# The opening of a two-block layer kernel: zero matmuls between the halves of x, short loads on ScalarE's queue, and the first norm's sums moved into the second weight chunk

## The reference, cut to what matters

```
def _rmsnorm(x, w):
    xf = x.astype(jnp.float32)
    y = xf * lax.rsqrt(jnp.mean(xf * xf, axis=-1, keepdims=True) + RMS_EPS)
    return (y * w.astype(jnp.float32)).astype(x.dtype)
...
    h = jnp.concatenate([meta, x], axis=1)
...
    h = h + _mixer(_rmsnorm(h, norm_mix_w[l]), w_in[l], ...)
...
    proj = u @ w_in
    rq, rk, rv, rg, a_cq, a_ckv, a_kr, a_gret, a_gmla = jnp.split(proj, SPLIT_IDX, axis=-1)
```

## Time and profile before

| | |
|---|---|
| time, three runs | 1061.37 us median (1061.02 to 1061.76) |
| the profiled execution | 1061.51 us, span 1059.7 us |
| mean granted TensorE clock | 0.997 |
| busy over the span | PE 1041.0 us, PEld 963.7, DVE 745.9, ACT 548.0, POOL 2.2 |
| HBM read | 174.78 MB, 166 GB/s over the span |

### The profile page before, as it was taken

How to read it: one execution, slowest core, us unless ns; L and a number is a source line. 1 busy time by engine, 2 the same in 40 slices (tenths; PEclk the granted TensorE clock), 3 DMA queues, 4 the chain that set the end, 5 groups by cost and what they waited for, 6 DMA issues and landing times.

```text
span 1059.7 us, 19331 instructions
## 1 busy us (share of the span) xinstructions
PE 1041.0 (98%) x7716; PEld 963.7 (91%) x7716; DVE 745.9 (70%) x810; ACT 548.0 (52%) x589; POOL 2.2 (0%) x5
## 2 busy tenths in 40 slices
PE   8999999999999999999999999999999999999998
PEld 7998997899999999989889999999898997888887
DVE  6855747768766666678767766666788987766673
ACT  6422536545644444465796444444576574444442
POOL 0000000000000000000000000000000000000000
PEclk8999999999999999999999999999999999999999
DMA  9894242345556666666416455465353444646531
GB/s 304 234 205 147 80 140 80 120 140 166 170 173 180 191 195 196 186 201 224 134 41 238 159 195 201 158 207 190 120 160 120 163 156 158 236 160 204 192 119 40
DMA packets 162589, 177.11 MB, mean 167 GB/s; under 512 B 4800, under 2 KB 148288, under 8 KB 162536
## 3 DMA queue, kind: packets, MB, share of 16 engines
q1 hardware_dynamic: 160704, 174.06, 51.5%
q10 hardware_dynamic: 1832, 2.30, 1.2%
HBM read 174.78 MB, written 1.57 MB: 166 GB/s over the span
## 4 chain that ended last, share of the span: by engine, by line
PE 82%; DVE 11%; ACT 4%; issue 1%; DMA 1%; SPq 0%; DVEq 0%; ACTq 0%
PE proj L466 38%; PE aux L910 13%; PE proj L476 11%; PE aux L932 8%; PE proj L475 5%; DVE wlo L1727 4%; DVE f L1727 2%; DVE f L1730 2%; ACT whi L1244 1%; DVE u L1730 1%; PE aux L663 1%; DVE x_all L1727 1%; DMA f<-in_x_dram 1%; PE aux L778 1%; PE aux L763 1%
## 5 line engine op out<-in xcount | busy, mean ns | idle before, releaser
L1727 DVE TENSOR_TENSOR wlo<-raw,whi 128x2048 fp32r<-128x2048 f32 (+2 forms) x179 | 374.6, 2093 | 100.8 <-ACT whi L1244 88.5
L466 PE MATMUL proj<-u,whi 128*128 128x256 f32 (+1 forms) x1888 | 345.4, 285 | 1.5 <-DVE u L1730 0.7
L1244 ACT ACTIVATE whi<-raw 128x2048 fp32r<-128x2048 f32 (+2 forms) x172 | 309.6, 1800 | 69.4 <-PE proj L466 41.9
L466 PEld LDWEIGHTS proj<-u,whi 128*128 128x128 f32 x1888 | 291.5, 189 | 8.3 <-issue 6.5
L466 PE MATMUL proj<-u,wlo 128*128 128x256 f32 (+1 forms) x944 | 266.2, 282 | 0.0
L476 PE MATMUL proj<-u,whi 128*128 128x512 f32 x512 | 179.7, 393 | 0.0
L466 PEld LDWEIGHTS proj<-u,wlo 128*128 128x128 f32 x944 | 178.5, 189 | 0.0
L910 PE MATMUL aux<-v,whi 128*128 128x256 f32 x864 | 154.3, 280 | 0.8 <-DVE v L1727 0.8
L475 PE MATMUL proj<-u,wlo 128*128 128x256 f32 x512 | 143.7, 281 | 0.9 <-DVE u L1730 0.9
L910 PEld LDWEIGHTS aux<-v,whi 128*128 128x128 f32 x864 | 133.0, 188 | 1.9 <-issue 1.2
L910 PE MATMUL aux<-v,wlo 128*128 128x256 f32 x432 | 120.9, 280 | 0.0
(11 more groups left out here) (307 smaller groups left out, 1065.2 us busy)
## 6 DMA issues: line engine op xcount, KB each, us to landing
raw<-in_mlp_w_dram SPq DMA_DIRECT2D x64, 1024.0 KB, 5.5
raw<-in_w_in_dram SPq DMA_DIRECT2D x21, 1024.0 KB, 7.5
raw<-in_od_w_in_dram SPq DMA_DIRECT2D x12, 1024.0 KB, 5.3
raw<-in_w_ffn_gate_dram SPq DMA_DIRECT2D x22, 512.0 KB, 3.9
raw<-in_w_ffn_up_dram SPq DMA_DIRECT2D x22, 512.0 KB, 5.2
raw<-in_w_ffn_down_dram SPq DMA_DIRECT2D x21, 512.0 KB, 5.4
raw<-in_ev_w_in_dram SPq DMA_DIRECT2D x10, 1024.0 KB, 5.5
raw<-in_w_ret_out_dram SPq DMA_DIRECT2D x4, 1024.0 KB, 5.3
```

The lines of the kernel that those rows point to most:

```text
L466: ins = mm(o, w_of(a, k), x_of(b, k), start=first and k == 0 and j == 0, stop=last and k == kt - 1 and j == 2, skip_group_check=skip)
L1244: A.post(act(slot(whi, n, 0, wd), slot(raw, n, 0, wd), ACT.Copy), "hi_ready")
L1727: return ve.tensor_tensor(o, a, b, op)
```

## The change

It does five things, all within the first tens of microseconds:

1. Seven matmuls on zeros (`FILL = 7`, the same instruction as the ten at the start) stand between the turning of k = 3 and of k = 4, ahead of the wait for the right half of x.
2. The 16-row pieces of x (the meta tokens and the tail, of each half) are issued on ScalarE's queue, behind the identity; the parameters follow between the two halves.
3. VectorE keeps the copies of groups 2 and 3 later: the low parts of u and of chunk 0's right half go ahead of them. After chunk 0 it keeps 4 and 5, splits chunk 1, keeps 2, 3, 6 and 7, and splits chunk 2 ahead of the three small operations on the gains.
4. ScalarE squares groups 0 and 1 ahead of chunk 1, groups 4 and 5 ahead of chunk 2, the rest behind it.
5. TensorE's partial sums move from ahead of rq1 to between its two column blocks, and the sum over them from k = 4 of the first block to k = 4 of the second.

```diff
+FILL = 7
@@
             for half, x_sem, w_sem in ((0, "x_left", "first_left"), (1, "x_right", "raw_landed0")):
                 c = slice(512 * half, 512 * half + 512)
-                sp.dma_start(x_tok[0:META, 0, c], meta[:, c]).then_inc(sems[x_sem], 16)
                 sp.dma_start(x_tok[META:P, 0, c], x[0:P - META, c]).then_inc(sems[x_sem], 16)
                 sp.dma_start(x_tok[:, 1, c], x[P - META:2 * P - META, c]).then_inc(sems[x_sem], 16)
-                sp.dma_start(x_tok[0:META, 2, c], x[S - META:S, c]).then_inc(sems[x_sem], 16)
@@
-                                   lambda a, k: src[:, a, k, t0:t0 + t], kt, gate=gate if j == 0 else None)
+                                   lambda a, k: src[:, a, k, t0:t0 + t], kt, gate=gate if j == 0 else late_gate)
@@
             for k in range(KT):
+                if k == 4:
+                    for j in range(FILL):
+                        mm(proj[:, 0, 0:P], warm, warm, start=True, stop=True)
                 if k % 4 == 0:
                     pe.wait_ge(sems["x_right" if k else "x_left"], 64)
@@
-            pe.wait_ge(sems["x_ready"], KT)
-            pe.wait_ge(sems["sq_ready"], 4)
-            for k in range(KT):
-                part = slice(32 * (k % 4), 32 * (k % 4) + 32)
-                ins = mm(aux[part, 0, 0:L], C("ones")[:, 0:32], sq[:, k, :], start=k < 4, stop=k >= 4, skip_group_check=True)
-            ins.then_inc(sems["sum_parts"], 1)
+
+            def token_parts():
+                pe.wait_ge(sems["x_ready"], KT)
+                pe.wait_ge(sems["sq_ready"], 4)
+                for k in range(KT):
...
+                ins.then_inc(sems["sum_parts"], 1)
@@
-            project("rq1", t0=META, t=S, gate=token_sums)
+            project("rq1", t0=META, t=S, between=token_parts, late_gate=token_sums)
@@
-            nc.scalar.dma_start(par[:, :], params).then_inc(sems["par_in"], 16)
+            for half, x_sem in ((0, "x_left"), (1, "x_right")):
+                c = slice(512 * half, 512 * half + 512)
+                nc.scalar.dma_start(x_tok[0:META, 0, c], w["meta_tokens"][:, c]).then_inc(sems[x_sem], 16)
+                nc.scalar.dma_start(x_tok[0:META, 2, c], w["x"][0][S - META:S, c]).then_inc(sems[x_sem], 16)
+                if half == 0:
+                    nc.scalar.dma_start(par[:, :], params).then_inc(sems["par_in"], 16)
@@
+            def token_squares(c, kept):
+                eng.wait_ge(sems["x_ready"], kept)
+                A.post(act(sq[:, 2 * c:2 * c + 2, :], x_all[:, 2 * c:2 * c + 2, :], ACT.Square), "sq_ready")
+
+            token_squares(0, 2)
             pump(index["rq0"] - AHEAD + 1)
-            for c in range(4):
-                eng.wait_ge(sems["x_ready"], 2 * c + 2)
-                A.post(act(sq[:, 2 * c:2 * c + 2, :], x_all[:, 2 * c:2 * c + 2, :], ACT.Square), "sq_ready")
+            token_squares(2, 4)
             pump(index["rq0"] - AHEAD + 2)
+            token_squares(1, 6)
+            token_squares(3, 8)
@@
-            keep(2)
-            keep(3)
             for k in range(4, KT):
                 first_lo(k)
@@
             done[0] = 1
-            for k in range(4, KT):
+            keep(4)
+            keep(5)
+            pump(index["rq0"] - AHEAD + 1)
+            for k in (2, 3, 6, 7):
                 keep(k)
+            pump(index["rq0"] - AHEAD + 2)
             B.run(tt(both_gains, par[:, PAR_COLS["final"][0]:PAR_COLS["final"][0] + KT], both_gains, ALU.mult))
             final_gains = par[:, PAR_COLS["final"][0]:PAR_COLS["final"][0] + KT]
             B.run(tt(gains_and_eps, final_gains, final_gains, ALU.mult))
             B.run(ts(gains_and_eps, gains_and_eps, EPS, ALU.add))
-            pump(index["rq0"] - AHEAD + 2)
```

More of the change, by code:

```diff
@@ L493, in finish, with project @@
                 ins.then_inc(sems["chunk_used"], 1)
-            def project(name, blocks=2, src=u, t0=0, t=L, kt=KT, width=256, m=P, step=P, off=0, gate=None, between=None):
+            def project(name, blocks=2, src=u, t0=0, t=L, kt=KT, width=256, m=P, step=P, off=0, gate=None, between=None,
+                        late_gate=None):
                 n = index[name]
@@ L585, in _ @@
             finish(ins)
-            pe.wait_ge(sems["x_ready"], KT)
-            pe.wait_ge(sems["sq_ready"], 4)
-            for k in range(KT):
-                part = slice(32 * (k % 4), 32 * (k % 4) + 32)
-                ins = mm(aux[part, 0, 0:L], C("ones")[:, 0:32], sq[:, k, :], start=k < 4, stop=k >= 4, skip_group_check=True)
-            ins.then_inc(sems["sum_parts"], 1)
+            def token_parts():
+                pe.wait_ge(sems["x_ready"], KT)
+                pe.wait_ge(sems["sq_ready"], 4)
+                for k in range(KT):
+                    part = slice(32 * (k % 4), 32 * (k % 4) + 32)
+                    ins = mm(aux[part, 0, 0:L], C("ones")[:, 0:32], sq[:, k, :], start=k < 4, stop=k >= 4, skip_group_check=True)
+                ins.then_inc(sems["sum_parts"], 1)
             def token_sums(k):
```

## The result

The changed kernel takes **1065.13 us**, the median of 16 runs (1063.40 to 1065.77), against 1061.51 us for the kernel before in as many runs of the same series. The ratio is 1.0027 with a 95% interval of 1.0021 to 1.0034: slower by 0.27% (the two medians lie 3.62 us or 0.34% apart, since the median of the changed kernel falls into the upper of two groups of times). The forecast was 1061.2 with a range to 1063.3, so both the time and the sign are missed. The 16 executions lie in two groups, seven from 1063.4 to 1063.9 us (mean granted clock 0.998 to 1.000) and nine from 1064.9 to 1065.8 us (0.996 to 0.999). The profiled one took 1065.49 us, span 1063.7 (before: 1061.51 and 1059.7), and belongs to the upper group. Of all executions told in this document one was in a slow state, 1264.68 us at a mean clock of 0.753 in the run with the sum two steps earlier, and it is left out there.

What follows compares the result with a forecast made beforehand. The opening was taken to be bound by the chain from x's right half through TensorE to rk0's start. rk0 moving from 28.04 to 27.9, 0.14 us earlier, took the median of 1061.37 to 1061.2 us, range 1059.8 to 1063.3.

Steps and rivals of the forecast that it cites:

- everything hangs on rk0's start: Opening: the change is worth what it moves the start of rk0, from 28.04 to 27.9, 0.14 us earlier.
- The fill's price: Seven zero matmuls after the left half: 0.22 us each at full clock, 1.54 us, PE free at 9.78.
- the root would be late: End of rq1: sum ends 24.58, 3.26 us more to rq0's read-out at 27.84, while PE ends rq1 at 26.0.
- wait 1.9 us for `proj_free`: Between rq1 and rk0: PE idles 1.9 us from 26.0 until rq0 is read out, a wait not there before.
- the rival that this wait can drop the clock: Start of rk0: first 6 us at half pace after the 1.9 us wait, 3.1 us lost, 1064.3 us; chance 0.13.
- Loads: DMA issues of the opening: right half landed by 8.8, parameters at 5.8, left tail at 5.4, all in time.
- The four steps behind the partial sums: rq1's second block: partial sums end at 22.7, four steps of 0.356 us bring the sum's start to 24.12.
- a right half at 10.32: Bound of the forecast's case, transfer not earlier: ScalarE delayed by 0.54 us, rk0 at 28.4, 0.4 us lost.
- the signs that the prediction named for being right: Profile after: no PE idle 1.56 to 12, clock 1.00 from 9 to 17, rq0 done near 18, rk0 at 27.9.
- the second fall of the clock: Clock row between 26 and 34 us: a second fall there would show the forecast wrong.
- The rule that several issuing engines give no bandwidth: Loads: spreading DMAs over engines only saves issue time; by it the sum would be up to 0.5 us worse.

Runs made afterwards that it cites:

- Fill alone: The kernel before with only the seven zero matmuls ahead of the right half of x: 1060.79 us, ratio 0.9989.
- Loads alone: The kernel before with only the short pieces of x and the parameters moved on ScalarE's queue: 1062.63 us, ratio 1.0005.
- Norm alone: The kernel before with only parts three to five of the change, no fill and loads as before: 1064.65 us, median of six, ratio 1.003.

## Why the prediction was wrong

**Right, and confirmed by runs.** That everything hangs on rk0's start: it came 2.45 us later, and the span followed with the clock's 1.6 on top. The fill's price in the changed kernel: 0.12 us a pass at full clock (8.11 to 9.77 in 14 passes) where 0.11 was said, the right half at 9.77 where 9.78 was forecast. That the root would be late and TensorE would wait 1.9 us for `proj_free`: 2.00 in the changed kernel, and 1.31 when the sum was set two steps earlier. And the rival that this wait can drop the clock, priced at 3.1 us: it did in the profiled execution and, by the two groups and the run with zeros in the wait, in about nine of sixteen, at 1.6 us, not 3.1, since the fall came 1.3 us into rk0 and only 3.4 us ran at half pace. It had a chance of 0.13. The list of waits spoke against it with idle times of up to 1.4 us; the one fall in the trace stood behind 2.13, and 2.0 was nearer to that.

**The step that failed** is one sentence under "Loads": the parameters, "issued near 2.1 with 3.7 us to landing, come at 5.8, also ahead of 6.78", and "these cost nothing under that cover; each us past it would be a us". The issue time was right, the landing was not: 6.4 us, at 8.6. The 3.7 came from a DMA that stood second on its queue and was issued at 1.2; it was carried over to one that stands fourth, is issued at 2.15, and meets larger pieces that SP now issues earlier. The left tail with the same 3.7 took 4.2 and was just in time. For the right half, the text took 5.78 us, the dearest row, as a bound; for the parameters and the left tail, where the cover ended 1 us and 0.6 us later, it took the cheapest and gave no bound at all. With 5.78 on an issue at 2.15 the parameters come at 7.9, past the cover, and 1.1 us of loss would have stood in the sum as a bound.

From there the loss can be followed through the forecast's own terms. ScalarE started 1.88 us late. VectorE's left low half ended at 13.63 instead of 11.74, chunk 1's low part at 20.31 instead of 18.76: 1.55 us. PE, which now stood 1.7 us in two waits, was given the lower clock near 14.7 and reached rq1 only at 20.99, 0.7 us behind the low part. From there to rk0 it took 9.5 us where the working has 9.1. rk0: 30.49 instead of 27.9, which is these three together.

The last of them is a **second term, mis-sized**. The four steps behind the partial sums were priced at 4 x 0.356 = 1.42 us, although show 1.58 for the same twelve matmuls, and the hand-overs around the sums were left out. From rq1's start to rk0's the runs took 9.50 us in the changed kernel, 9.58 with only the right short pieces moved, and 9.61 with the old loads. So the loads are not the whole miss. For a right half at 10.32 the prediction had rk0 at 28.4 and 0.4 us lost; with the old loads the right half's turning began at 10.52, rk0 came at 29.08, and the median was 1.2 us above its reference, a part of it from executions in which the clock fell.

Of the signs that the prediction named for being right, only the wait ahead of rk0 and the fill's price came. There was idle time between 5 and 12 us, the clock was down from 14.7 to 18.1, rq0 ended near 21 and not near 18, and the second fall of the clock, which it named as a sign of being wrong, came at 31.8.

**The weighing of the two rules.** The rule that several issuing engines give no bandwidth (the Trainium skill, DMA: Bandwidth & Descriptors, "Rules for kernel authors") was read as a limit on the gain. Here it bore on the cost: DMA moved 383 GB/s in the microsecond from 3 to 4 us against 283 before, but 168 against 266 in the one ahead of it, and the short pieces took longer on the second queue than they had on SP's, 4.7 against 3.5 us in the median for the meta tokens and 5.2 against 4.7 for the tails. The same page ("Queues, rings and completion order") says that each DMA engine takes packets from the queue rows in turn; the trace agrees with that in so far as both queues were served at once, but a short piece gained little by it against the large one of the same moment: 4.2 us against 5.5 at 1.69 (32 and 512 KB), 5.8 against 6.2 at 2.69 (32 and 256 KB), and 6.4 against 5.8 at 2.15 (69.5 and 224 KB), where it came last. Whether the packets of the other queue or the pieces' own size make them slow, no run here tells apart.

**The parts, by the runs.** Fill alone: -1.0 us. Loads alone: +0.8. Norm alone: +2.8. Together +3.6 in the medians (+2.0 for the lower group, whose median is 1063.54). The sum of the three is 2.6; what is over lies in how they meet, and the runs do not split it. A part may be the fall near 14.7 us: it comes behind the two gaps that the late parameters open in TensorE, though the fill had held the clock until then.

## What to carry to other kernels

A transfer's time to landing belongs to when and where it is issued and to what else is in flight, not to its size alone (the same 69.5 KB took 3.7, 4.9 and 6.4 us here): before moving a DMA, take the dearest row of the trace for anything whose cover is under two microseconds, and ask it of every piece that is pushed back by the move. When the sums of a late-applied norm are moved behind a block of matmuls, count the chain from the sum to the first read-out against the matmuls left behind it; here 3.3 us stood against four steps of 0.36. And a new wait of one to two microseconds on TensorE should be priced with the clock behind it, or filled.

## What the hardware showed that was not expected

By the two groups of times, the same idle time of 2.0 us brought the clock down in about nine executions of sixteen and not in the rest, with nothing else different in the kernel, and eight zero matmuls in it (0.24 us each) removed the difference: 1063.36 to 1064.28 in eleven executions. The profiles show both outcomes directly: behind the 2.0 us ahead of rk0 the clock fell in the changed kernel, with only the right short pieces moved and with the old loads, and it did not with the parameters first nor with the norm's move alone.

Shorter idle times went ahead of a fall too. With the loads alone the clock fell within an idle time of 1.13 us, behind the turning of the left half, and with the sum two steps earlier it fell near 13.6 us, some 2.3 us behind one of 1.04 us, the longest between the first matmul and the fall. The idle times of up to 1.4 us that did nothing in the kernel before are thus no safe bound for the opening. In the run with the parameters first, the clock fell right behind the start of the fill (0.60 on average from 10 to 11 us), behind an idle time of 1.76 us and 2.1 us of turning, so a fill placed behind such an idle time came too late and ran at 0.22 us a pass.

```profile
10.00:11.00 1.00, 1.00 (x6) 0.97 (x7) 0.93 (x3) 0.94 (x3) 0.00 (x0) 0.60 1.09 345
```

Two more 32 KB pieces on the other queue went with 1.0 us more to landing for the left tail on SP's queue (4.7 against 3.7 us, issued at 2.13 both times), in one profiled execution. In the profiles with the loads of before it took 3.5 to 4.0 us.
